# Differential attention: fp32 score matmuls exchanged for three passes over split operands

## The reference, cut to what matters

```
q = rms_norm_gain(q.reshape(b, n, 8, 2, 64), q_norm_g)      # the same for k; then rope_2d on the latent tokens
s = einsum('bqhmd,bkhmd->bhmqk', q, k) * scale               # m: the two maps
p = softmax(s);  p = p[:, :, 0] - lam * p[:, :, 1]
o = einsum('bhqk,bkhv->bqhv', p, v)                          # 128 value features a head
```

## Time and profile before

| | us |
|---|---|
| median of 3 runs | 3007.77 (3007.25 to 3009.14) |
| the profiled execution, own time | 3006.21 |
| its span, first to last instruction | 3004.4 |
| TensorE busy in the span | 2949.9 (98%) |
| last value group (g=4) and 16 rounds of attention | about 949.7 to 1015.2 |

### The profile page before, as it was taken

One profiled execution on the slowest core, in us unless ns is written; L12 is line 12 of the kernel. 1 busy time (PEld: TensorE's weight loads), 2 busy tenths in 40 slices (PEclk: granted clock), 3 DMA queues, 4 the chain that ended last, 5 costly groups with the idle time before them and its releaser, 6 DMA issues.

```text
span 3004.4 us, 40234 instructions
## 1 busy us (share of the span) xinstructions
PE 2949.9 (98%) x14353; PEld 2420.3 (81%) x14353; DVE 2129.7 (71%) x3282; ACT 1192.7 (40%) x1803; POOL 193.5 (6%) x163
## 2 busy tenths in 40 slices
PE   7999999999999999999999999999999999999998
PEld 5888678888887789977888888788888888876787
DVE  6973688877786788699898876566754632756875
ACT  3223524332143664556441323443244422423443
POOL 2300000000001000000040210000000000002120
PEclk9999999999999999999999999999999999999999
DMA  7672065666633156311266552672366622452554
GB/s 276 200 245 92 21 197 174 215 202 240 205 102 112 57 182 222 129 57 43 99 208 212 175 183 76 213 248 100 102 219 215 215 91 92 150 188 95 199 186 144
DMA packets 125230, 479.26 MB, mean 160 GB/s; under 512 B 13752, under 2 KB 13752, under 8 KB 122768
## 3 DMA queue, kind: packets, MB, share of 16 engines
q1 hardware_dynamic: 119232, 443.60, 44.5%
q0 software_dynamic: 5840, 33.51, 3.1%
HBM read 459.23 MB, written 17.83 MB: 159 GB/s over the span
## 4 chain that ended last, share of the span: by engine, by line
PE 79%; issue 10%; DVE 6%; ACT 2%; DMA 1%; SPq 0%; POOL 0%; DVEq 0%; ACTq 0%; POOLq 0%
PE bank L798 21%; PE bank L800 21%; PE bank L799 21%; PE bank L811 4%; PE bank L812 2%; PE bank L1727 2%; PE bank L1100 1%; DVE x_res L2667 1%; DVE w_lo L2551 1%; PE bank L810 1%; DMA ada_first<-in_ada 1%; DVE x_res L2673 1%; PE bank L1206 1%; ACT w_hi L1795 1%; DMA ml_v<-v_spill 0%
## 5 line engine op out<-in xcount | busy, mean ns | idle before, releaser
L2551 DVE TENSOR_TENSOR w_lo<-w_raw,w_hi 128x1024 fp32r<-128x1024 f32 x617 | 754.7, 1231 | 498.1 <-ACT w_hi L1795 489.1
L1795 ACT ACTIVATE w_hi<-w_raw 128x1024 fp32r<-128x1024 f32 x620 | 649.5, 1055 | 755.6 <-PE bank L800 626.4
L798 PE MATMUL bank<-h_hi,w_hi 128*128 128x512 f32 (+1 forms) x1432 | 524.5, 366 | 7.3 <-DVE h_lo L2640 5.2
L799 PE MATMUL bank<-h_lo,w_hi 128*128 128x512 f32 (+1 forms) x1432 | 518.9, 362 | 0.0
L800 PE MATMUL bank<-h_hi,w_lo 128*128 128x512 f32 (+1 forms) x1432 | 518.8, 362 | 0.0
L798 PEld LDWEIGHTS bank<-h_hi,w_hi 128*128 128x128 f32 x1432 | 270.4, 189 | 54.9 <-issue 9.7
L799 PEld LDWEIGHTS bank<-h_lo,w_hi 128*128 128x128 f32 x1432 | 270.4, 189 | 43.7 <-issue 1.2
L800 PEld LDWEIGHTS bank<-h_hi,w_lo 128*128 128x128 f32 x1432 | 270.3, 189 | 41.6
L798 PE MATMUL bank<-w_hi,xm_hi 128*128 128x512 f32 x512 | 201.0, 393 | 0.1
L800 PE MATMUL bank<-w_hi,xm_lo 128*128 128x512 f32 x512 | 199.4, 389 | 0.0
L799 PE MATMUL bank<-w_lo,xm_hi 128*128 128x512 f32 x512 | 199.3, 389 | 0.0
(11 more groups left out here) (473 smaller groups left out, 5667.3 us busy)
## 6 DMA issues: line engine op xcount, KB each, us to landing
w_raw<-in_weights SPq DMA_DIRECT2D x620, 512.0 KB, 4.2
ada_ring_f<-in_ada SPq DMA_DIRECT2D x56, 512.0 KB, 3.4
ada_ring_g<-in_ada SPq DMA_DIRECT2D x44, 512.0 KB, 3.4
ada_ring_b<-in_ada SPq DMA_DIRECT2D x38, 512.0 KB, 4.2
ada_ring_a<-in_ada SPq DMA_DIRECT2D x32, 512.0 KB, 3.4
ada_first<-in_ada SPq DMA_DIRECT2D x16, 512.0 KB, 15.3
v_spill<-ml_v POOLq DMA_DIRECT2D x4, 1024.0 KB, 6.9
o_spill<-ml_o_grp POOLq DMA_DIRECT2D x4, 1024.0 KB, 4.6
```

The lines of the kernel that those rows point to most:

```text
L798: mm(out, lhs[0], rhs[0], start=start, stop=False)
L799: mm(out, lhs[0], rhs[1], start=False, stop=False)
L1795: return nc.scalar.activation(out, in_, func, **kw)
L2551: V.tensor_tensor(WLO[:, slot, :], RAW[:, slot, :], WHI[:, slot, :].bitcast(F32), SUB)\
```

## The change

The scores are no longer fp32 matmuls but the same three passes as in the projections. For each round there are six float32r matmuls of 64 rows x 512 columns: high x high for both maps, high query x low key for both, low query x high key for both, with each map in a bank of its own. For this the queries and keys are split. ScalarE copies `DQ` to a new buffer of high parts `DQHI` in four pieces of 128x512 (`q_high`), behind the copies of g=0; and `DK` to `DKHI` in eight pieces of 128x512 (`k_high`), behind the copies of g=2 and ahead of the value copies of g=3. GpSimd subtracts the high parts from `DQ` and `DK` where they stand (`DQLO` and `DKLO` are the same memory), in four and eight pieces, behind its DMA of the context and ahead of the small factors. `DCOL`, a buffer of columns, moves by 4 KiB to make room. `d_scores` waits for the low part of its head in addition.

```diff
+        DKHI = at("diff_k_hi", [P, 8, TOK], ARENA + 48 * K, F32R)
+        DQHI = at("diff_q_hi", [P, 8, LAT], ARENA + 88 * K, F32R)
+        DQLO = at("diff_q_lo", [P, 8, LAT], ARENA, F32R)
+        DKLO = at("diff_k_lo", [P, 8, TOK], ARENA + 8 * K, F32R)
+
+        def q_pair(T, b):
+            return T[:, 2 * b:2 * b + 2, :].rearrange("p h n -> p (h n)")
...
             pool.dma_start(X[:, :, LAT:TOK], ctx2_t).then_inc(S("x_in"), 16)
+
+            for b in range(4):
+                pool.wait_ge(S("d_hi_done"), N("d_hi_done", b + 1))
+                pool.tensor_tensor(q_pair(DQLO, b), q_pair(DQ, b), q_pair(DQHI, b).bitcast(F32), SUB)\
+                    .then_inc(S("d_lo_done"), 1)
+            for h in range(DIFF_HEADS):
+                pool.wait_ge(S("d_hi_done"), N("d_hi_done", 4 + h + 1))
+                pool.tensor_tensor(DKLO[:, h, :], DK[:, h, :], DKHI[:, h, :].bitcast(F32), SUB)\
+                    .then_inc(S("d_lo_done"), 1)
...
-                for m in range(2):
-                    part = slice(64 * m, 64 * (m + 1))
-                    mm(PS[D_SCORE[u % 2][m]][:, :], DQ[part, h, t * P:(t + 1) * P], DK[part, h, :],
-                       start=True, stop=True).then_inc(S("d_score"), 1)
+                if t == 0:
+                    pe.wait_ge(S("d_lo_done"), N("d_lo_done", 4 + h + 1))
+                for i in range(3):
+                    for m in range(2):
+                        part = slice(64 * m, 64 * (m + 1))
+                        q = (DQLO if i == 2 else DQHI)[part, h, t * P:(t + 1) * P]
+                        k = (DKLO if i == 1 else DKHI)[part, h, :]
+                        last = mm(PS[D_SCORE[u % 2][m]][:, :], q, k, start=i == 0, stop=i == 2)
+                        if i == 2:
+                            last.then_inc(S("d_score"), 1)
...
+            def q_high():
+                for b in range(4):
+                    f(q_pair(DQHI, b), q_pair(DQ, b), ACT.Copy).then_inc(S("d_hi_done"), 1)
+
+            def k_high():
+                for h in range(DIFF_HEADS):
+                    f(DKHI[:, h, :], DK[:, h, :], ACT.Copy).then_inc(S("d_hi_done"), 1)
...
                 d_copies(g)
+                if g == 0:
+                    act.wait_ge(S("dtok_copy"), 4)
+                    q_high()
+            act.wait_ge(S("dtok_copy"), 12)
+            k_high()
             v_copies(3)
```

More of the change, by code:

```diff
@@ L129 @@
           "d_std": ("silu_c_done", 3),
+          "d_hi_done": ("qk_lat", 16), "d_lo_done": ("log_gamma_done", 1),
           "d_inverse": ("score_done", 3 * RET_HEADS),
@@ L286, in program @@
         DLAM = at("diff_lam", [P, 256], ARENA + 86 * K)
-        DCOL = at("diff_col", [P, 256], ARENA + 88 * K)
+        DCOL = at("diff_col", [P, 256], ARENA + 84 * K)
+        DKHI = at("diff_k_hi", [P, 8, TOK], ARENA + 48 * K, F32R)
[4 more added lines that the diff above has]
+            return T[:, 2 * b:2 * b + 2, :].rearrange("p h n -> p (h n)")
         def d_root(g, i, n=1):
```

## The result

The changed kernel takes 3011.49 us (median of 20 runs, 3009.75 to 3014.24), against 3007.07 us for the kernel before in 20 runs on the same chip (3005.16 to 3009.14). The ratio is 1.0016, 95% interval 1.0009 to 1.0022: 4.4 us longer, which is inside the 0.2% that I counted as no change, but outside my range of 3004.8 to 3010.3. The profiled execution took 3010.23 us, with a span of 3008.4, 4.0 more than before's.

The account below looks back on a forecast made before the run. TensorE, busy 98% of the span, was taken to bound the kernel. Scores -1.9, ScalarE copies +0.05 and VectorE's hold-up +1.25 gave -0.6 us, from 3007.77 to 3007.2 us; range 3004.8 to 3010.3.

Parts of the forecast that it names:

- The scores: Attention rounds on TensorE: a round's score group falls from 1.06 to 0.89 us, 1.9 us gained in all.
- the 0.21 around a group: Score group: 0.21 us for the exposed first load and emptying the array, the same before and after.
- the ScalarE loop: Rounds: loop through scores, VectorE, ScalarE's copy and values takes over as bound, two rounds going from 5.08 to 4.85 us.
- value loads waiting for ScalarE's copy: Attention rounds: expected sign of the loop as bound, TensorE's value load waiting for ScalarE's copy; no size given.
- Copies on ScalarE: Four query and eight key copies: 0.05 us lost for the queries' overrun, nothing for the keys.
- GpSimd's work as work: Four query and eight key subtractions on GpSimd, 1.36 us each, cost nothing as work.
- Who waits gets the turn before the other's next instruction: VectorE and GpSimd at 936.2: tile 18's `w_lo` waits for one subtraction, so TensorE stands and 1.25 us are lost.
- VectorE first: Rival, chance 0.25: VectorE gets in ahead of GpSimd at 936.2, tile 18 is in time, 3005.9 us.

Follow-up runs that it names:

- gated: Changed kernel with GpSimd waiting, ahead of its four query subtractions, until VectorE has made the low part of tile 20: 3004.65 us, ratio 0.9994.
- fp32_gated: `gated` with scores as two fp32 matmuls a round on the high parts, low parts made but left out: 3006.37 us, ratio 1.0000.
- dma_behind: Changed kernel with GpSimd's DMA of the context issued behind all twelve subtractions: 3005.42 us, one run, beside 3006.46 of before.
- memset_for_dma: Changed kernel with GpSimd's DMA behind all twelve subtractions and a 128x1000 memset in its old place: 3005.60 us, one run, beside 3006.62 of before.
- after_add: Changed kernel with GpSimd waiting, between its DMA and the query subtractions, for the end of VectorE's last addition only: 3004.01 us, one run.
- two_then_gate: Changed kernel with two query subtractions behind the DMA and the other two held until tile 20's low part is made: 3008.74 us, one run.
- fp32_scores: Changed kernel with scores as two fp32 matmuls a round on the high parts, low parts made but left out: 3016.02 us, ratio 1.0028.
- delayed: Changed kernel with three tiny memsets of four columns on GpSimd between its DMA and the query subtractions: 3013.29 us, one run.
- late: Changed kernel with one 128x512 memset on GpSimd between its DMA and the query subtractions: 3013.75 us, one run.
- reordered: `gated` with ScalarE's copy of round u-2 put ahead of the two exponentials of round u: 3001.26 us, ratio 0.9981.
- serial: `gated` with the score loops exchanged, three passes of one map and then three of the other: 3005.82 us, one run.

## Why the prediction was wrong

**The scores: right, in every term that was measured.** The group went to 0.89 us as summed; the loads of the second and third step don't show, the maps run side by side; the ScalarE loop took over and two rounds are 4.87 us (I had 4.85); the gain is 1.9 us, by the offsets in the trace and, independently, by `gated` against `fp32_gated`. What the 0.21 around a group is made of (first load, emptying the array) no run shows; it stayed as large as before. One detail differed: I had expected the wait to stand in a row of value loads waiting for ScalarE's copy; it shows mainly as value pieces of 1.01 us, every second round.

**Copies on ScalarE: right.** Next to nothing, and `fp32_gated` at 1.0000 has them all.

**GpSimd's work as work: right.** A subtraction is 1.22 us to my 1.36, none of the scores waited for one, and the eight of the keys held VectorE for 0.7 to 1.1 us three times, but for nothing that TensorE was waiting for.

**"Who waits gets the turn before the other's next instruction": this step failed.** I took it from the earlier trace rows, where GpSimd runs two instructions in a row or one, and none of them behind a DMA of its own. It holds for `dma_behind`, `memset_for_dma` and `after_add`, and the price that I put on it (1.25) is what `memset_for_dma` shows (1.1). But behind the DMA, with GpSimd never idle, VectorE got no turn until GpSimd's last subtraction was through. From that one step came both errors of the sum:
- *the size*: not one subtraction but four, 4 x 1.22. TensorE stands 5.4 us longer than before, and `two_then_gate` shows that the length is that of GpSimd's run;
- *the victim*: I looked at the `w_lo` of tile 18, as the instruction ready when GpSimd's DMA ended. It was the instruction ahead of it, the addition. I had taken it to run to its end at 936.32; in the changed kernel its record begins 0.6 us ahead of the first subtraction, and it was held all the same.

**Left out: the clock.** Some 5.7 us of idle TensorE was followed by 3.4 us at the lower level, 1.1 us more. I had not priced what a stall brings with it, and it can be more: in the profiles of `fp32_scores`, `delayed` and `late`, with the same hold, it was 6.8 us at the lower level. At the length that I had expected it brings nothing: `memset_for_dma` waits 1.1 us and has the granted clock at 1.00 in 935 to 950 us, while `two_then_gate`, with 3.2 us, has 0.91 and 0.87 in 935 to 942 and 942 to 950.

So -1.9 + 0.05 + 1.25 = -0.6 should have been -1.9 + 0 + 5.4 + 1.1 = +4.6, against 4.4 measured in the medians (the 1.1 is of one profile, so the closeness of the two is partly luck). Of the rivals none was this case; "VectorE first" describes the kernel with the wait (3005.9 predicted, 3004.65 and 3004.01 measured on other chips). My range treated one subtraction as the upper end of this term. The diff has four in a row, and the honest upper end was four.

The Trainium skill has a lock that fits this: "SBUF — State Buffer", section "Who interferes with whom", says that a VectorE instruction with two SBUF inputs contends with a GpSimd one that reads SBUF. The runs agree (the addition takes 0.69 us free and 1.65 in `dma_behind`). On one point they go further: the page speaks of one instruction's length, and here it was the length of an uninterrupted run of four.

**Open.** Why the DMA matters: the runs show that it does, and that 0.2 us of an idle GpSimd behind it is enough to undo it, but not by what mechanism. The DMA's 1 MB takes 6.1 us to land in the changed kernel and 6.0 in `after_add`, so its data in flight don't do it alone. No run has another transfer size either. Open too are up to 1.2 us of `fp32_scores`, and part of what `reordered` wins.

## What to carry to other kernels

Work that is moved to an idle GpSimd isn't free if it reads SBUF beside VectorE instructions with two SBUF inputs: find which of these TensorE waits for at that time, and price the hold at one GpSimd instruction, but right behind a DMA that GpSimd issues at its whole unbroken run. A wait for the critical VectorE instruction cost nothing here, where GpSimd had slack, and was worth some 6.7 us. Where a loop through two engines sets the pace, look in the list of the other engine for work that stands ahead of the late instruction without being needed by it: with two calls exchanged the ratio to the kernel before went from 0.9994 (interval up to 1.0003) to 0.9981 (up to 0.9990).

## What the runs showed of the hardware that I had not expected

- VectorE's addition, 0.69 us long, was held for 6.06 us behind a GpSimd DMA and four GpSimd subtractions with no gap, and 3.64 us with two. With a `memset` instead of the DMA, or 0.21 us of idle GpSimd, the engines took turns of one instruction.
- Matmuls of 64 rows in different row halves overlapped also where kernel.py's list has all of one half's ahead of the other's (`serial`: 0.90 us for six; not shown is whether the engine got them in that order). Only a wait between them made them serial, 0.91 to 0.96 for each three.
- The loads of a second and third pass in the same rows are hidden: the passes follow each other at 0.23 us. The Trainium skill, "TensorE: Matmul & The Clock Gate", section "The mechanism", ties this overlap to a change of row group in its list of what overlaps, and above it also names a background weight buffer. By the first the group would have stayed near 1.06; it is 0.89, which agrees with the second.
- After 5.7 us without a matmul, TensorE was at the lower level for 3.4 us in one profile (the changed kernel) and for 6.8 in another (`fp32_scores`), with the same hold ahead; `delayed` (5.8 us idle) and `late` (5.2) had 6.8 as well. After 3.2 us it was there for (7 x 0.09 + 8 x 0.13) / 0.5 = 3.3 us, after 1.1 us not at all.
- The lower level also came without any wait ahead: in ten of the fourteen profiles, but not in before's or the changed kernel's, TensorE has 3.4 us of it between 2640 and 2663 us, in unchanged code. In `gated` TensorE was busy 6.00 of 6.00 us ahead of it (2636 to 2642), and the kernel loses 1.5 us there against before. So spans of single profiles differ by this much for no reason of the change. `gated`, 2642 to 2650 us:

```profile
2642.00:2650.00 8.00, 8.00 (x45) 6.51 (x44) 1.50 (x3) 1.65 (x4) 0.00 (x0) 0.79 0.33 121
```
